# Eight token-major linear layers computed by one level of Strassen's scheme

## The reference, cut to what matters

```python
u = rmsnorm(h, g_norm)                                  # (256, 1024)
rq, rk, rv, rg, gqkv, gz, ... = jnp.split(u @ w_in, SPLIT_IDX, axis=-1)
v = rv.reshape(B, T, RET_HEADS, RET_DV)                 # values of the retention
y_ret = (o.reshape(B, T, RET_V) * silu(rg)) @ w_br_ret  # gate of the retention
y_gdn = (o.reshape(B, T, GDN_V) * silu(gz)) @ w_br_gdn  # gate of the delta rule
# and in the HGRN2 layer
q_raw, f_raw, v, g = split(u @ w_in)                    # v: values, g: gate (silu)
```

## Time and profile before

| what | value |
|---|---|
| median of 3 runs | 3016.78 us (3015.39 to 3021.06) |
| the profiled execution | 3015.04 us |
| its span, first to last instruction | 3013.2 us |
| mean granted TensorE clock, as a share of 2.4 GHz | 0.969 |
| PE busy | 2831.3 us, 94% |
| PEld busy | 2411.2 us, 80% |
| DVE busy | 1034.5 us, 34% |
| ACT busy | 463.1 us, 15% |
| POOL busy | 167.3 us, 6% |

### The profile page before, as it was taken

The page is one execution under the profiler, slowest core; times in us unless marked ns, Lnnn a source line. Parts: engine busy times, 40 slices in busy tenths (PEclk is TensorE's granted clock), DMA queues, the critical chain, the costliest instruction groups (busy, mean ns, idle before and its releaser), DMA issues.

```text
span 3013.2 us, 37613 instructions
## 1 busy us (share of the span) xinstructions
PE 2831.3 (94%) x16558; PEld 2411.2 (80%) x16558; DVE 1034.5 (34%) x1507; ACT 463.1 (15%) x720; POOL 167.3 (6%) x154
## 2 busy tenths in 40 slices
PE   7999899999999989999999999799699899995998
PEld 5778788999676878899997887576599777765997
DVE  2333224565243222434220000323455541335332
ACT  0161110001125111100000000121210111122101
POOL 0002210000000321000000000000000010000000
PEclk9999999999999999899999999899799999997999
DMA  6432216766443212344447878432276734431451
GB/s 239 140 126 85 69 58 216 259 252 226 148 139 126 70 57 85 133 143 154 175 150 239 290 264 280 159 126 98 67 277 256 260 116 139 138 112 56 149 179 64
DMA packets 211952, 476.11 MB, mean 158 GB/s; under 512 B 7632, under 2 KB 36944, under 8 KB 211536
## 3 DMA queue, kind: packets, MB, share of 16 engines
q1 hardware_dynamic: 211072, 469.27, 45.1%
q10 hardware_dynamic: 720, 4.46, 0.4%
HBM read 472.64 MB, written 1.05 MB: 157 GB/s over the span
## 4 chain that ended last, share of the span: by engine, by line
PE 84%; issue 10%; DVE 4%; ACT 1%; POOL 1%; DMA 0%; POOLq 0%; SPq 0%; DVEq 0%; ACTq 0%
PE ps L423 28%; PE ps L1347 16%; PE ps L435 10%; PE ps L1488 9%; PE ps L1678 7%; PE ps L1707 3%; PE ps L870 1%; PE ps L881 1%; PE ps L877 1%; PE ps L1717 1%; DMA ring<-in_w_in 0%; PE ps L1895 0%; PE ps L764 0%; PE ps L2113 0%; PE ps L495 0%
## 5 line engine op out<-in xcount | busy, mean ns | idle before, releaser
L423 PE MATMUL ps<-uT,ring 128*128 128x256 f32 x2816 | 631.1, 383 | 28.1 <-DMA ring<-in_w_in 16.4
L423 PEld LDWEIGHTS ps<-uT,ring 128*128 128x128 f32 x2816 | 537.0, 192 | 105.3 <-issue 22.2
L1488 PE MATMUL ps<-work,ring 128*128 128x256 f32 x1584 | 344.9, 379 | 0.0
L1488 PEld LDWEIGHTS ps<-work,ring 128*128 128x128 f32 x1584 | 299.7, 190 | 39.9
L435 PE MATMUL ps<-ring,uT 128*128 128x512 f32 x704 | 305.6, 595 | 0.0
L435 PEld LDWEIGHTS ps<-ring,uT 128*128 128x128 f32 x704 | 133.9, 191 | 164.9 <-issue 164.7
L1678 PEld LDWEIGHTS ps<-work,ring 128*128 128x128 f32 x1760 | 198.6, 192 | 5.1 <-issue 4.8
L1678 PE MATMUL ps<-work,ring 128*128 128x128 f32 (+4 forms) x1760 | 198.4, 275 | 0.0
L1347 PE MATMUL ps<-uT,ring 128*128 128x128 f32 x1584 | 190.2, 279 | 3.2 <-ACT uT L618 2.5
L1347 PE MATMUL ps<-xn,work 128*128 128x128 f32 x1584 | 184.9, 280 | 7.8 <-issue 7.8
L1347 PEld LDWEIGHTS ps<-uT,ring 128*128 128x128 f32 x1584 | 186.8, 196 | 6.0 <-issue 5.3
(11 more groups left out here) (369 smaller groups left out, 2864.8 us busy)
## 6 DMA issues: line engine op xcount, KB each, us to landing
ring<-in_w_in SPq DMA_DIRECT2D x72, 1024.0 KB, 5.0
work<-in_ada_w SPq DMA_DIRECT2D x48, 1024.0 KB, 9.2
ring<-in_exp_w_down SPq DMA_DIRECT2D x40, 1024.0 KB, 5.0
ring<-in_attn_w_in SPq DMA_DIRECT2D x36, 1024.0 KB, 5.1
ring<-in_exp_w_gate SPq DMA_DIRECT2D x32, 1024.0 KB, 6.3
ring<-in_exp_w_up SPq DMA_DIRECT2D x32, 1024.0 KB, 5.6
ring<-in_ffn_w_in SPq DMA_DIRECT2D x32, 1024.0 KB, 5.3
ring<-in_ffn_w_out SPq DMA_DIRECT2D x20, 1024.0 KB, 5.2
```

What stands on the lines that cost most here:

```text
L423: mm = pe.matmul(acc[:, m * T:(m + 1) * T], w[:, k, m * P:(m + 1) * P], src[:, half * 4 + k, :], start=(half == 0 and k == 0 and m % 2 == ...
L1488: mm = pe.matmul(bank[2 + n // 4][:, n % 4 * T:(n % 4 + 1) * T], w[:, k, n * P:(n + 1) * P], hid[g][:, t0 + k, :], start=False, stop=True, ...
```

## The change

All eight layers are computed by one level of Strassen's scheme in the form with seven products of 512 x 512 weights with 512 features x 128 tokens, instead of eight. With A the four blocks of the weight and B the four blocks of the tokens, the token sums are T1 = B12 - B11, T2 = B22 - T1, T3 = B22 - B12, T4 = T2 - B21; the weight sums are S1 = A21 + A22, S3 = A11 - A21, S2 = S1 - A11, S4 = A12 - S2.

- `quad_pe` takes the two units of a layer at once and issues products P4, P1, P2, P5, P6, P3, P7, of four matmuls with 512 moving columns each. P6 and P7 accumulate onto P1 in one bank, P3 onto P5 in another.
- `quad_sums_dve`: four DVE additions of 128 x 2048 write each sum over a slab of the ring. Part 0 (S1) waits until P4 is done, part 1 (S3) for part 0, part 2 (S2) until P1 is done, part 3 (S4) until P2 is done. P5 waits for part 0, P6 for part 2, P3 for part 3.
- `quad_snaps`: four ACT copies of 128 x 512 keep P4, P1, P5 and P1+P6 (P6 waits for P1's, P3 for P5's, P7 for P6's).
- `quad_add_dve`: four DVE additions of 128 x 512 make the four blocks of the result. The gates' Silu is then one ACT operation of 128 x 2048 in SBUF, after `quad_done`.
- `token_quad_dve`: once for each of the three inputs, four DVE operations of 128 x 512.
- The slabs are loaded in another order (lower right, upper left, lower left, upper right), and come free later: one at P6, one at P3, two at the end of P7.
- The first two steps of the retention, s0 and s1, now stand between P6 and P3 of `rg`. On DVE, the sums of `rv` stand between the two rotations; `gz`'s parts 0 and 1 stand before the decay gates' first addition (L1095), parts 2 and 3 after their last one (L1102). In HGRN2 they stand among the operations on `hf`.

```diff
-            for j in range(2):
-                linear_n(pe, f"rv{l}", f"rv{l}{j}")
-            for j in range(2):
-                linear_n(pe, f"rg{l}", f"rg{l}{j}")
+            quad_pe(pe, f"rv{l}", True, sums_ready=TQ_AT[name])
+            quad_pe(pe, f"rg{l}", True, before_last=lambda: retention_pe(pe, l, RET_ORDER[0:2]))
+            retention_pe(pe, l, RET_ORDER[2:])
...
-            for j in range(2):
-                linear_n(pe, f"gz{l}", f"gz{l}{j}")
+            quad_pe(pe, f"gz{l}", True)
...
+            for what in order:
+                if what == "P4":
+                    if sums_ready is not None:
+                        pe.wait_ge(tq_ready, sums_ready)
+                    slab_wait(pe, at["A22"])
+                    product(what, d, weights("A22"), T4, True)
+                elif what == "P1":
+                    product(what, a, weights("A11"), B11, True, None if first is None else 0)
+                elif what == "P2":
+                    product(what, b, weights("A12"), B21, True, None if first is None else 4)
+                elif what == "P5":
+                    pe.wait_ge(q_sum, 4 * Q + 1)
+                    product(what, c, weights("A22") if s1 is None else ..., T1, True)
+                elif what == "P6":
+                    pe.wait_ge(q_sum, 4 * Q + 3)
+                    pe.wait_ge(q_snap, Q_SNAPS * Q + 2)
+                    product(what, a, weights("A11"), T2, False, None, True)
+                elif what == "P3":
+                    pe.wait_ge(q_sum, 4 * Q + 4)
+                    pe.wait_ge(q_snap, Q_SNAPS * Q + 3)
+                    if before_last is not None:
+                        before_last()
+                    product(what, c, weights("A12"), B22, False, None, True)
+                else:
+                    pe.wait_ge(q_snap, Q_SNAPS * Q + 4)
+                    product(what, a, weights("A21"), T3, False)
...
# mixer_dve
+            token_quad_dve(dve, f"mix{l}")
+            rope_dve(dve, 2 * l, qk_ret[:, 0:1024], col("sin1"), 64, rbs)
+            for part in range(4):
+                quad_sums_dve(dve, f"rv{l}", part)
+            rope_dve(dve, 2 * l + 1, qk_ret[:, 1024:2048], col("sin1"), 64)
+            for which in ("11", "12", "21"):
+                quad_add_dve(dve, f"rv{l}", which, snap_buffers(8), v_ret)
...
             unit_norm(3)
+            quad_sums_dve(dve, f"gz{l}", 0)
+            quad_sums_dve(dve, f"gz{l}", 1)
             acc = full(dve, f"ab{l}")
...
             dve.wait_ge(g_ready, l + 1)
+            quad_sums_dve(dve, f"gz{l}", 2)
+            quad_sums_dve(dve, f"gz{l}", 3)
+            for which in ("11", "12", "21", "22"):
+                quad_add_dve(dve, f"gz{l}", which, snap_buffers(0), o_gdn)
             for t in range(TT):
                 unit = f"v{l}{t}"
...
# mixer_act, after the decay gates' Sigmoid
+            quad_snaps(act, f"gz{l}", snap_buffers(0))
+            quad_done(act, f"gz{l}")
+            act.activation(o_gdn, o_gdn, ACT.Silu).then_inc(tick(gz_out), 1)
```

More of the change, by code:

```diff
@@ L243, in linear, with quad @@
                         wide(name, w, half * 512, 4, c0 + j * 512, 512)
+            def quad(name, w, c0):
+                for j, half in ((1, 1), (0, 0), (1, 0), (0, 1)):
+                    wide(name, w, half * 512, 4, c0 + j * 512, 512)
             def halves(name, w):
@@ new lines, in quad_phases, with phase_wait, snap_buffers, quad_snaps @@
+        def quad_phases(slab):
+            return (("P1", "P2", "P4") if quad_at[slab][4] else ("P4", "P1", "P2")) + ("P5", "P6", "P3", "P7")
+        def phase_wait(eng, slab, what):
+            if what == "P7":
+                eng.wait_ge(slab_used, quad_at[slab][0]["A12"] + 1)
+            else:
+                eng.wait_ge(q_phase, Q_PHASES * quad_no[slab] + quad_phases(slab).index(what) + 1)
+        def snap_buffers(k0):
+            return [area(k0 + 0.5 * i, 512) for i in range(4)]
+        def quad_snaps(act, slab, snaps, which=("P4", "P1", "P5", "P6")):
+            Q = quad_no[slab]
+            _, u0, u1, _, first = quad_at[slab]
+            if Q and "P4" in which:
+                act.wait_ge(q_out, 4 * Q)
+            where = {"P4": (0, u1[:, 512:1024]), "P1": (1, u0[:, 0:512]), "P5": (2, u1[:, 0:512]), "P6": (3, u0[:, 0:512])}
+            for what in quad_phases(slab):
+                if what in which:
+                    i, acc = where[what]
+                    phase_wait(act, slab, what)
+                    act.activation(snaps[i], acc, ACT.Copy).then_inc(tick(q_snap), 1)
@@ L916, in mixer_act @@
                 rope_act(act, 2 * l + j, f"rqk{l}{j}")
[L917 to L926, removed]
+            quad_snaps(act, f"rv{l}", snap_buffers(8))
+            quad_snaps(act, f"rg{l}", snap_buffers(8))
+            quad_done(act, f"rg{l}")
+            act.activation(o_ret, o_ret, ACT.Silu).then_inc(tick(ret_g), 1)
             for j in range(6):
@@ L1036, in mixer_dve @@
                 unit = f"ret{what}{l}"
+                if what == "o0":
+                    for which in ("12", "21", "22"):
+                        quad_add_dve(dve, f"rg{l}", which, snap_buffers(8), o_ret)
                 acc = full(dve, unit)
@@ L2088, in hgrn_pe @@
                 linear_t(pe, "hf", f"hf{j}")
[L2089 to L2092, removed]
+            quad_pe(pe, "hv", True, sums_ready=TQ_AT["smix0"])
+            quad_pe(pe, "hgt", True)
             pe.wait_ge(hg_mul, 6)
@@ L2163, in hgrn_act @@
                 free(unit)
+            quad_snaps(act, "hv", snap_buffers(20), ("P4", "P1"))
             for j in range(2):
@@ L2172, in hgrn_act @@
                 act.activation(flat(ke, j), flat(ke, j), ACT.Exp).then_inc(tick(hg_exp), 1)
[L2173 to L2176, removed]
+            quad_snaps(act, "hgt", snap_buffers(20))
+            quad_done(act, "hgt")
+            act.activation(hg, hg, ACT.Silu).then_inc(tick(hg_gt), 1)
             for t in range(TT):
@@ L2212, in hgrn_dve @@
                                   bj[:, :, HG_C - 1:HG_C].broadcast_to([P, 4 * NC, HG_C]), bj, ALU.subtract).then_inc(tick(hg_b), 1)
+            for which in ("12", "21", "22"):
+                quad_add_dve(dve, "hv", which, snap_buffers(20), hv)
+            dve.wait_ge(q_out, 4 * (quad_no["hv"] + 1))
+            dve.nop().then_inc(tick(hg_v), 1)
+            for part in range(4):
+                quad_sums_dve(dve, "hgt", part)
             for j in range(2):
```

162 lines of the change are left out of this document (143 added, 19 removed).

## The result

The changed kernel takes 2996.82 us (median of 4 runs, 2992.43 to 3000.85) against 3018.87 us (4 runs): a ratio of 0.9929, 95% interval 0.9914 to 0.9944, or 22 us less. A second set of runs gave 2994.23 against 3016.90 us, ratio 0.9923 (0.9909 to 0.9936). The profiled execution took 2998.65 us with a span of 2996.9 us.

The account below looks back on a forecast made before the run. PE was taken to bound the kernel, with 84% of the chain. Two mixers' rv and rg -13.6, two gz +7.2 and HGRN2 -6.4 gave -12.8 us; forecast 3004.0 us, range 2994 to 3012 us.

Parts of the forecast that it names:

- rival A: Wait in gz too short to lower the clock, all else as forecast: -18.8 us, 2998.0 us; chance 0.23.
- 4 matmuls are 3.43 us, pitch unchanged: Each of eight layers drops from 32 to 28 matmuls on PE: 3.43 us less a layer, 27.5 us at most.
- The chain of sums has 3.4 us of slack: Within a layer, PE waits for weight sums only where DVE comes more than 3.4 us late.
- rival B: Weight sums far slower than 2.29 us; at 4.6 us a sum the kernel becomes slower, 3033 us; chance 0.07.
- The ring: Weight slabs land 5.0 us after request; even at twice that nothing waits, so costed at nothing.
- rival C: The ring starves: slabs take 10 us or more, PE waits some 2 us at five places; 3014 us; chance 0.08.
- `gz` waits 3.3 us before P6 for ACT's chain: In each gz the third sum stands behind ACT's Abs to Sigmoid; PE's wait takes back the whole 3.43 us.
- The clock: Behind each gz wait, 6.8 us at half speed, a loss of 3.0 us; bounds 0 and 4.7 us.
- the 0.4 us: At HGRN2's end the Silu and ACT's copy of kn finish late for L2121: 0.4 us lost.
- the token sums were taken at 0.69 us each: Four DVE additions before P4, 2.8 us in all; in rv they shift the first rotation's end to 45.1.
- the idle of 3 to 3.7 us: Sign of being right: one such PE idle before P6 of each gz, ended by DVE, then granted clock 0.50.
- the transposes behind `gz` come sooner: Sign of being wrong: they come sooner than before relative to L771; each gz was forecast +0.6 us before the clock.

Follow-up runs that it names:

- e4_slow_sums: Changed kernel with an extra, unused DVE addition of 128 x 2048 before each weight sum of rv and rg in both mixers; 3007.82 us, ratio 0.9969.
- e1_gates_first: Changed kernel with the decay gates' first addition before the four weight sums in both gz, their last two steps after; 2990.43 us, ratio 0.9910.
- e3_longer_wait: Changed kernel with two extra, unused DVE additions of 128 x 512 before the third weight sum of each gz; 3002.77 us, ratio 0.9946.
- e9_retention_plain: Changed kernel with rv and rg of both mixers back to plain matmuls, gz and HGRN2 as changed; 3011.29 us, ratio 0.9974.

## Why the prediction was right, and where its size was off

- The mechanism was right: faster, by products saved, at six layers of eight. -12.8 us was forecast, and 22 measured. The time is nearest to rival A (2998.0 us, the clock stays), which had less than half the chance of the forecast, and it is inside the range because the range reached down to A.
- *4 matmuls are 3.43 us, pitch unchanged*: the stretch of `rv` and `rg` is 6.8 us shorter in both mixers, as forecast, and plain layers in their place cost 14.5 us.
- *The chain of sums has 3.4 us of slack*: borne out by `e4_slow_sums` (10 to 11 expected, 11.0 measured); by the trace it is 3.0 us before P6 and 4.0 before P3, since the sums stand 2.4 us apart and not 2.3. The sums took 2.29 to 2.34 us in the mean, so rival B falls. In `hv`, the tightest place, 0.9 us was forecast: the third sum ended at 2019.25, and P6 was due at 2020.12.
- *The ring*: no wait of PE for a slab in any of the eight layers; rival C falls.
- *`gz` waits 3.3 us before P6 for ACT's chain*: 3.04 us in the first, and it took the 3.4 us back; 1.34 us in the second. Part 2 was forecast 14.8 us behind `gz`'s start (218.9 less 204.11), and is 14.7 behind it. The place was shown by `e1_gates_first`. What was read right here was an order: DVE was idle most of the time, and PE waited for it.
- **The step that was mis-sized is "The clock"**: "I take a stretch of 6.8 us at half speed for each `gz`", 3.0 us each. After 3.04 us of idle the clock stayed at 1.00 in both sets of runs: 0 in place of 6.0 us. The bound of 0 stood in the text, and the value was taken from the nearer rows (3.82, 3.92 us), which stood among other work. Even where a longer wait did lower the clock here, it was for 3.4 us and cost 1.6 to 1.7.
- Smaller: the second `gz` already had low clock behind L771, and I carried it over as a constant. It now overlaps the wait, and this `gz` is 1.8 us shorter (1.7 of it by the overlap) and not 0.6 us longer. 2.4 us of the difference are from there. The first `gz` cost 0.1 and not 0.6 us. In HGRN2 ACT's copies of `kn` ended 0.1 us before L2317 was due, so the 0.4 us were not lost: -6.8 instead of -6.4 us. (The -6.4 has a rounding in it: -6.9 + 0.4 is -6.5.)
- Together: 6.0 + 2.4 + 0.5 + 0.4 = 9.3 us, the difference between 12.8 and 22.1.
- Of no effect: the token sums were taken at 0.69 us each. The first of them took 2.30 us beside POOL's rotation step (2.37 in the second mixer), but the first step of the rotation behind them took 2.45 us instead of 4.14. So DVE was done at 45.47 instead of 45.1, and its first weight sum began at 51.82.
- Of the signs set down beforehand these did not come: the idle of 3 to 3.7 us in the second `gz`, and a granted clock of 0.50 behind either. And one sign of being wrong did: the transposes behind `gz` come sooner after L771 (now L961) than before, 30.91 us against 31.04 in the first mixer and 30.90 against 32.74 in the second. The 1.8 us of the second mixer are the low clock that the wait took in, which the prediction had not seen.

The Trainium skill's rule (TensorE: Matmul & The Clock Gate, section "Part 1: The HAM clock gate"), that the slow clock is what the array falls back to without activity, agrees with the waits of 4.08 and 5.06 us here. At 3.04 us the slow clock did not come, so the +3.6 us that the prediction drew from this rule did not come either.

## What to carry to other kernels

When one engine bounds a kernel and another has room, cost added work on the second by its place in that engine's queue: at six layers 12 us of vector work hid under 24 us of matmuls, at two the same work stood behind a round trip to ACT, and the wait took back all that the saved matmuls were worth. Put the first step of such a round trip ahead of long independent work, and its last step behind it. Price a wait of a few microseconds by itself first; a fall of the clock behind it is a second, uncertain price, and a low clock that is there already may end up inside the wait.

## What the runs showed of the hardware that was not expected

POOL's broadcasts of the decay (`bc`, two copies of 128 x 512 from a small tile) took 1.16 us before and 5.35 us in the changed kernel, where DVE runs weight sums at the same time; with the gates first, where no weight sum stands beside them but an addition with one input in PSUM (L593), they take 1.16 us again. Rows of POOL in the changed kernel, and in the one with the gates first:

```profile
212.34 5.35 POOL L1464 COPY work<-tiny 128x512 f32<-128x512 f32 x2 [89.29 <-DVE tiny L1299]
```

```profile
213.10 1.16 POOL L1462 COPY work<-tiny 128x512 f32<-128x512 f32 x2 [90.36 <-DVE tiny L1299]
```

DVE is held up too: L576 took 2.48 us beside them, and L571 in `e3_longer_wait` 2.58 us, against 2.29. Nothing waits for these copies before the solve, so it cost nothing here. The Trainium skill (SBUF — State Buffer, section "SBUF: two separate sides") says that a DVE operation with two SBUF inputs and a GpSimd operation that reads SBUF shut each other out for whole instructions; the long copies, which read `tiny` in SBUF, agree with it.

The same shows at the rotation. Its first step on DVE (L675, now L859, two operations) took 4.14 to 4.16 us before the change in both passes of both mixers, each time with POOL's step of the rotation (L666, now L850) beside it. In the changed kernel it takes 2.45 us. In the first pass the first token sum now stands beside POOL's step, and it is that sum which is long: 2.30 and 2.37 us in the two mixers, 0.63 us in HGRN2, where POOL is idle. In the second pass POOL's step (49.49 to 51.49) is over before the weight sums begin at 51.82, and the rotation comes behind them. `e9_retention_plain`, without these sums, has both cases in one kernel: 2.45 us in the first pass, 4.16 in the second. First the changed kernel, then `e9_retention_plain`:

```profile
36.11 2.30 DVE L620 TENSOR_TENSOR xn<-uT 128x512 f32<-128x512 f32 x1
...
40.49 2.45 DVE L859 TENSOR_TENSOR work<-work,small 64x1024 f32<-64x1024 f32 x2
```

```profile
48.52 4.16 DVE L859 TENSOR_TENSOR work<-work,small 64x1024 f32<-64x1024 f32 x2 [3.98 <-ACT work L844]
```

```profile
48.56 3.03 POOL L850 TENSOR_TENSOR work<-work,small 128x1024 f32<-128x1024 f32 x1 [11.63 <-ACT work L844]
```

So the added 1.6 to 1.7 us belong to whichever of these operations of DVE meets POOL's step, and not to the rotation. It cost nothing here, since DVE was ahead of PE in both places.
